# A hybrid S5 / forgetting-attention / mixture-of-experts block: router, sorting step, tail and the down product of the 144-column passes rearranged

## The chip, the cores and the metric

The kernel runs on one core of a Trainium2 chip. The metric is the device time of one execution in microseconds; lower is better. Engines: TensorE (PE, with its weight loads PEld), VectorE (DVE), ScalarE (ACT), GpSimd (POOL) and SyncE (SP), which issues most of the DMAs.

## The reference

For 1024 tokens of width 1024, all in float32:

```python
x = x + concat(rmsnorm(attn), rmsnorm(ssm)) @ w_out          # attention heads and state-space heads
h = rmsnorm(x, norm_ffn_g)
logits = h @ w_router + b_router                             # 32 experts
top_val, top_idx = lax.top_k(logits, 4);  gates = softmax(top_val)
y[e] = (clamped_swiglu(h_rows_of_e @ w_gu[e] + b_gu[e])) @ w_dn[e] + b_dn[e]
x = x + sum over the 4 chosen experts of gate * y
x = x + sigmoid(rmsnorm(x, norm_ple_g) @ w_ple_gate) * (p @ w_ple_proj)
out = rmsnorm(x, norm_final_g)
```

The 4096 (token, expert) rows are grouped by expert; each expert has weights of 8 MB (gate and up) and 4 MB (down).

## The kernel before

The work is written out by hand, engine by engine: each engine has one program, and semaphores (`wait_ge`, `then_inc`) order them. `link` on VectorE and GpSimd makes the next instruction wait for the one before. The stages touched here are these.

**Output projection and router (433 to 570 us).** Eight row tiles `t` of 128 tokens. On TensorE `attn_part` (L1766) and `ssm_part` (L1771) make two 512-column products per half tile, in two PSUM banks; `resid` on VectorE (L1279, L1280) scales each by its row's reciprocal norm and adds it to `x1`, both after `wo_mm`, which the second product signals. `norm_rows` and ScalarE's `ffn_norm` (L806) form the RMS norm and `hn` (L1289). SP stores each `hn` tile to the DRAM table `normalised_rows` (L397) and, for tiles 0 to 5, reads it back in quarters `hq` (L403), from which VectorE's `router_turn` makes the transposed tile `h2T`. Tiles 6 and 7 are transposed on TensorE (`turn_rows`, L1785) and copied by ScalarE (`router_in`, L813). `route` (L1795) multiplies `h2T` as 128-column weights with 128 moving columns of the router weights, placed so that the last 32 are the logits. `logits` (L1293 to L1306) adds the bias, takes the top values and indices and builds the one-hot tiles `oh` and `sel`.

**Sorting step (570 to 616 us).** VectorE counts the rows of each expert (L1343 ff.) and chooses for each a pass width from `WIDTHS = (96, 112, 120, 128, 144, 192, 224, 256)`; `first_ready` gives the first expert to SP, which then loads four of its gate/up chunks (L408). VectorE goes on to each row's place (L1378 to L1391) and makes one-hot tables `ohr`, `ohc` in four quarters (L1395, L1396). ScalarE scales them by token numbers (`tokens_in`, L855) between its other copies (`gates_in` L834, `gates_turned` L841, `bias_out` L847), and TensorE sums them (L1866): the result is the list of row ids. Meanwhile VectorE makes the pass table (L1401 to L1421), which SP copies to `passrow` (L418) for every engine's loop bounds. `rowid` and `rowq` (L1425 to L1427) turn the ids into gather indices; GpSimd gathers the first rows in four indirect DMAs (`gather`, L607); the wait on `rows0_ld` then releases the other gate/up chunks on SP (L437 ff.) and the first turn `xT` on VectorE (L1450). The slot numbers for the final gather (L1432 to L1438) are made ahead of that turn.

**Expert passes (616 to 2103 us).** One loop per width. The passes of 96 (`narrow_pass`) use the tokens as 32-column weights (L1958, L1985), four strips at a time. All others (`expert_pass`) use gate/up weights as the stationary operand and `xT` as the moving one (L1894, or L1897 in 64-column halves up to width 128), and then, for the down product, `actT` as the stationary operand and 512 columns of `wd` as the moving one, for each half `c` all eight `f` (L1911), with a second form for tokens past 128 (L1916, L1924, L1936). There are 6 passes of 96, 8 of 112, 5 of 120, 2 of 128, 7 of 144, 3 of 192 and one each of 224 and 256. VectorE and ScalarE evacuate each `f` (L1497, L1498, L921, L1487, L1490); ScalarE copies the output to `yb` (`y_out`, L876 ff.); GpSimd stores it (`serve_pass`) and gathers rows two passes ahead (`gather_pass`). SP loads each chunk when its predecessor's last reader has signalled `gu_mm` or `dn_mm` (L443 to L450).

**Tail (2103 to 2266 us).** TensorE multiplies the per-layer input (L2023); GpSimd gathers four expert rows per token (L691); VectorE `combine` (L1510) adds them; ScalarE `ple_norm` (L927), TensorE `turn_tail` (L2030), ScalarE `gate_in` (L933), TensorE `gate` (L2039), ScalarE `ple_gate` (sigmoid, L940), VectorE `finish` (L1528, L1529) and `fin_norm` (L944 square, L946 square root) follow, and L1536 makes the output tile. VectorE combines tile `t + 2` ahead of finishing tile `t`.

Of the kernel before, what the change touches and what calls it, by code (L numbers as in the profile page):

```python
# [31 lines left out]
P = 128  # L32
# [13 lines left out]
E = 32  # L46
# [4 lines left out]

GR = 32
# [16 lines left out]
N_SMALL = 1092  # L69
# [36 lines left out]
def build(nc, x_cm, x_tm, pT, small, consts, b_f, d_skipT, b_router, gains, w_in, w_glu, w_out,  # L106
          w_router, w_router_q, w_gu, w_dn, b_exp, b_gu, b_dn, w_ple_gate, w_ple_proj, out, hs, ys, cum):
    with ExitStack() as ctx:
# [166 lines left out]
        slf = at("slf", [P, 32], F32, o); o += 128  # L275
        csel = at("csel", [P, 9, 32], F32, R_V + 32768)
        before = at("before", [1, 32], F32, R_V + 33920)
        assert o <= R_S
# [8 lines left out]
        wd = at("wd", [P, 2, FT, 512], F32, R_H + 65536)  # L287
# [16 lines left out]
        gdT = at("gdT", [P, 2, P], F32, R_S + 32768)  # L304
# [14 lines left out]
        sqj = at("sqj", [P, D], F32, o); o += 4096  # L319
        assert o <= R_C  # L320
# [20 lines left out]
        def _(sp):  # L341
# [89 lines left out]
            def dn_chunk(e, j):  # L431

                sp.dma_start(wd[:, j // 2, 4 * (j % 2):4 * (j % 2) + 4], w_dn[bass.ds(e, 1), j].rearrange("o p f m -> (o p) f m")
                             ).then_inc(S(f"dn_ld{j}"), 16)
# [22 lines left out]
            for t in range(8):  # L457
                sp.wait_ge(S("o_ready"), t + 1)
                sp.dma_start(out[:, t, :], ot[:, t % 2, :]).then_inc(S(f"o_st{t % 2}"), 16)
            sp.wait_ge(S("o_st0"), 64)  # L460
            sp.wait_ge(S("o_st1"), 64)
# [3 lines left out]
        def _(pool):  # L465
# [149 lines left out]

            pool.wait_ge(S("hs_st"), 16 * 8)
            pool.wait_ge(S("first_ready"), 1)
# [3 lines left out]

            pool.wait_ge(S("rowid_ready"), 2)
            gather(0, rowq)
# [26 lines left out]
            def serve_pass(b, narrow):  # L650
# [12 lines left out]
                if narrow:  # L663
                    for j in range(4):
                        pool.dma_start(ys[bass.ds(r0, WIDTHS[0]), 256 * j:256 * j + 256].rearrange("(r t) c -> t r c", t=GR),
                                       yb[GR * j:GR * j + GR, 0, 0:256 * NGR].rearrange("t (r c) -> t r c", c=256)).then_inc(S("y_st"), 16)
                else:
# [12 lines left out]
            with pool.Fori(ends0, npass) as b:  # L680
# [6 lines left out]
            for t in range(8):  # L687
                if t >= 2:
                    pool.wait_ge(S("yg_used"), t - 1)
# [7 lines left out]
        def _(act):  # L697
# [104 lines left out]
            a.activation(rss[:, :], rss[:, :], ACT.Sqrt).then_inc(S("sd2_ready"), 1)  # L802
# [7 lines left out]
            def router_in(t):  # L810
                act.wait_ge(S("ht_mm"), t - 5)
                act.wait_ge(S("ht_evac"), t)
                a.activation(h2T[:, t % 2, :, :].rearrange("p k j -> p (k j)"), ps[:, 4:6, :].rearrange("p b n -> p (b n)"),  # L813
                             ACT.Copy).then_inc(S("ht_evac"), 1)

            for t in range(8):
                ffn_norm(t)
                if t >= 6:
                    router_in(t)
# [7 lines left out]
            act.wait_ge(S("hs_st"), 16 * 8)  # L827
# [42 lines left out]
            def y_out(b, w):  # L870
# [3 lines left out]
                for c in range(2):  # L874
                    act.wait_ge(S("dn_mm"), b * 4 + (2 * c + 2 if rest % P == 0 else 4))
# [41 lines left out]
            for c, w in list(enumerate(WIDTHS))[1:]:  # L917
                with act.Fori(ends[c - 1], ends[c]) as b:
# [3 lines left out]
                    y_out(b, w)  # L922
# [19 lines left out]
            def fin_norm(t):  # L942
                act.wait_ge(S("x3_half"), 2 * t + 2)
                a.activation(sqj[:, :], x1[:, t, :], ACT.Square, accum_out=rstd[:, t:t + 1]).then_inc(S("zs_ready"), 1)  # L944
# [22 lines left out]
        def _(dve):  # L967
# [303 lines left out]
            dve.wait_ge(S("sd2_ready"), 1)  # L1271
# [3 lines left out]
            def resid(t, n):  # L1275
                w = 2 * t + n
                dve.wait_ge(S("wo_mm"), w + 1)
# [851 lines left out]
```

## Time and profile before

| | us |
|---|---|
| median of 3 runs | 2288.71 (2288.33 to 2290.12) |
| the profiled execution's own time | 2268.03 |
| its span, first to last instruction | 2266.5 |
| PE / DVE / ACT / POOL busy | 2208.7 / 958.3 / 423.6 / 605.5 |
| mean granted TensorE clock | 0.994 of full speed |

In the rows "A <- B" in a form reads "tile written <- tiles read", for a matmul "result <- moving, stationary". One float32 matmul of the program is two MATMUL instructions in the trace. `[x <- E]` behind a row of the timeline is idle time of the engine before it and what ended it; a row that begins with two numbers gives start and duration in us.

### The profile page before, as it was taken

How to read it: one execution, taken by the hardware profiler on the slowest of the kernel's cores; microseconds unless marked ns; L12 is line 12 of the kernel's file. 1: busy time of each engine (PE TensorE's matmuls, PEld its weight loads, DVE VectorE, ACT ScalarE, POOL GpSimd, SP SyncE). 2: the span in 40 equal slices, each digit the busy share in tenths (PEclk: the TensorE clock that was granted, in tenths of full speed). 3: DMA queues.
4: the chain of work that ended last, by engine and by line, in shares of the span. 5: the costliest groups of instructions: out<-in, count | busy, mean ns of one | idle time of the engine just before them, and what ended most of it. 6: DMA issues, size and time to landing. Idle time of an engine off the chain costs nothing.

```text
span 2266.5 us, 48298 instructions
## 1 busy us (share of the span) xinstructions
PE 2208.7 (97%) x19138; PEld 1532.9 (68%) x19138; DVE 958.3 (42%) x2120; ACT 423.6 (19%) x873; POOL 605.5 (27%) x915
## 2 busy tenths in 40 slices
PE   8999999999699999999999999999999999999998
PEld 5555566545455577878787787888877888777443
DVE  4664477344743343434344343333332222212474
ACT  3110166301311111111111110111111100010344
POOL 0555588100223312121211212222123111111320
PEclk9999999999899999999999999999999999999999
DMA  5100011321499999999999999788877666543540
GB/s 201 43 25 6 25 56 38 163 74 60 156 405 399 399 408 416 368 353 358 348 339 337 343 330 339 261 317 319 309 293 273 256 250 241 223 159 138 200 155 37
DMA packets 103097, 533.67 MB, mean 235 GB/s; under 512 B 22516, under 2 KB 26404, under 8 KB 50924
## 3 DMA queue, kind: packets, MB, share of 16 engines
q1 hardware_dynamic: 76748, 465.57, 54.4%
q0 software_dynamic: 26272, 67.02, 8.5%
q8 instruction: 55, 0.90, 0.2%
q14 instruction: 22, 0.18, 0.0%
HBM read 498.02 MB, written 31.23 MB: 234 GB/s over the span
## 4 chain that ended last, share of the span: by engine, by line
PE 84%; DVE 6%; DMA 5%; ACT 2%; issue 1%; SPq 1%; POOL 0%; DVEq 0%; POOLq 0%; ACTq 0%
PE ps L1894 20%; PE ps L1897 17%; PE ps L1911 16%; PE ps L1661 5%; DMA wg<-in_w_gu 4%; PE ps L1958 3%; PE ps L1650 2%; PE ps L1771 2%; PE ps L1766 2%; PE ps L1936 2%; DVE x L1510 2%; PE ps L1680 1%; PE ps L1714 1%; PE ps L2039 1%; PE ps L1746 1%
## 5 line engine op out<-in xcount | busy, mean ns | idle before, releaser
L1894 PE MATMUL ps<-xT,wg 128*128 128x144 f32 (+3 forms) x3072 | 451.1, 310 | 0.0
L1894 PEld LDWEIGHTS ps<-xT,wg 128*128 128x128 f32 x3072 | 441.6, 190 | 12.9 <-issue 6.3
L1497 DVE TENSOR_SCALAR gb<-ps,bcur 128x256 f32<-128x256 f32 x216 | 104.6, 484 | 780.2 <-PE ps L1894 458.3
L1897 PEld LDWEIGHTS ps<-xT,wg 128*64 128x64 f32 x7680 | 383.3, 137 | 11.0 <-issue 11.0
L1897 PE MATMUL ps<-xT,wg 128*64 128x112 f32 (+2 forms) x7680 | 386.7, 263 | 0.0
L1911 PE MATMUL ps<-wd,actT 128*128 128x512 f32 x864 | 376.9, 594 | 0.0
L1911 PEld LDWEIGHTS ps<-wd,actT 128*128 128x128 f32 x864 | 162.4, 190 | 196.1 <-issue 188.4
L921 ACT ACTIVATE sg<-gb 128x256 f32<-128x256 f32 x216 | 90.0, 417 | 731.5 <-DVE gb L1497 731.5
L607 POOL DMA_INDIRECT xg<-normalised_rows,rowc x184 | 177.9, 967 | 74.1 <-issue 45.7
L1958 PE MATMUL ps<-wg,xT 128*32 128x256 f32 x2304 | 133.7, 384 | 9.6 <-issue 6.9
L638 POOL COPY rowc<-rowq 128x8 uint32 (+1 forms) x34 | 6.3, 186 | 506.1 <-DVE xT L1450 506.1
L656 POOL DMA_DIRECT2D bin__182<-in_b_exp x33 | 18.9, 574 | 424.6 <-issue 298.1
L2039 PE MATMUL ps<-wpg,xnT 128*128 128x512 f32 x256 | 112.9, 595 | 6.1 <-ACT xnT L933 6.1
L1958 PEld LDWEIGHTS ps<-wg,xT 128*32 128x32 f32 x2304 | 73.3, 111 | 59.5 <-issue 15.2
L876 ACT ACTIVATE yb<-ps 128x512 f32<-128x512 f32 x54 | 31.1, 596 | 408.9 <-PE ps L1911 185.8
L1487 DVE TENSOR_TENSOR tb<-gb,sg 128x256 f32<-128x256 f32 x216 | 91.9, 426 | 34.8 <-ACT sg L921 34.8
L1498 DVE TENSOR_SCALAR ub<-ps,bcur 128x256 f32<-128x256 f32 x216 | 102.7, 475 | 0.0
L1490 DVE SCALAR_TENSOR_TENSOR actT<-ub,tb 128x256 f32<-128x256 f32 x216 | 91.7, 425 | 7.4
L2039 PEld LDWEIGHTS ps<-wpg,xnT 128*128 128x128 f32 x256 | 47.5, 190 | 65.9 <-issue 54.5
L1450 DVE STREAM_TRANSPOSE xT<-xg 128x1024 f32<-128x1024 f32 x61 | 72.4, 1221 | 1.6 <-DMA xg<-normalised_rows,rowq 1.6
L1985 PE MATMUL ps<-wd,actT 128*32 128x256 f32 x1152 | 64.6, 380 | 0.0
L670 POOL DMA_DIRECT2D expert_rows<-yb x48 | 34.9, 732 | 102.4 <-ACT yb L888 63.1
(413 smaller groups left out, 2415.6 us busy)
## 6 DMA issues: line engine op xcount, KB each, us to landing
wg<-in_w_gu SPq DMA_DIRECT2D x264, 1024.0 KB, 7.3
wd<-in_w_dn SPq DMA_DIRECT2D x132, 1024.0 KB, 7.8
expert_rows<-yb POOLq DMA_DIRECT2D x48, 256.0 KB, 8.5
expert_rows<-yb POOLq DMA_DIRECT2D x60, 128.0 KB, 4.8
hT<-in_x_cm SPq DMA_DIRECT2D x8, 512.0 KB, 9.5
cumb<-gate_sums SPq DMA_DIRECT2D x4, 1024.0 KB, 4.6
x<-in_x_tm SPq DMA_DIRECT2D x1, 4096.0 KB, 14.1
wout<-in_w_out SPq DMA_DIRECT2D x1, 4096.0 KB, 21.0
```

The lines of the kernel that those rows point to most:

```text
L607: g.indirect_dma_start(xg[:, half, DQ * r:DQ * r + DQ], None, hs[:, :], bass.IndirectOffsetOnAxis(ap=rows[:, r, half:half + 1], axis=0)).t ...
L921: a.activation(sg[:, f % 2, :], gb[:, f % 2, :], ACT.Sigmoid, scale=1.702).then_inc(S("sig_ready"), 1)
L1487: v.tensor_tensor(tb[:, f % 2, :], gb[:, f % 2, :], sg[:, f % 2, :], ALU.mult).then_inc(S("tb_ready"), 1)
L1490: v.scalar_tensor_tensor(actT[:, f, :], ub[:, f % 2, :], -6.0, tb[:, f % 2, :], ALU.max, ALU.mult).then_inc(S("act_ready"), 1)
L1497: v.tensor_scalar(gb[:, f % 2, :], ps[:, f % 2, 0:W], bcur[:, f:f + 1], 7.0, ALU.add, ALU.min).then_inc(S("g_ready"), 1)
L1498: v.tensor_scalar(ub[:, f % 2, :], ps[:, f % 2, W:2 * W], bcur[:, 8 + f:9 + f], 8.0, ALU.add, ALU.min).then_inc(S("gu_evac"), 1)
L1661: ins = m.matmul(ps[:, bank, :], w_[:, k, un[1] * P:un[1] * P + P], hT[:, k, 512 * un[2]:512 * un[2] + 512], start=(k == 0), stop=(k == KT ...
L1894: ins = m.matmul(ps[:, f % 2, g_ * W:g_ * W + w], wg[:, f, k, g_, :], xT[:, k, 0:w], start=(k == 0), stop=(k == KT - 1))
L1897: ins = m.matmul(ps[c:c + 64, f % 2, g_ * W:g_ * W + w], wg[:, f, k, g_, c:c + 64], xT[:, k, 0:w], start=(k == 0), stop=(k == KT - 1))
L1911: ins = m.matmul(ps[:, 2 + c, :], actT[:, f, 0:P], wd[:, c, f, :], start=(f == 0), stop=(f == FT - 1))
L1958: ins = m.matmul(ps[GR * j:GR * j + GR, ut % 2, 0:256], xT[:, k, GR * r:GR * r + GR], wg[:, f0:f0 + 2, k, j // 2, :], start=(k == 0), stop ...
L2039: ins = m.matmul(ps[:, 2 + n, :], xnT[:, t % 2, k, :], wpg[:, k, n * 512:n * 512 + 512], start=(k == 0), stop=(k == KT - 1))
```

## The change

- **Router.** `wa_mm` is new: `resid` adds the first product when it is done and the second after `wo_mm`. `route` uses the router weights as 32-column stationary tiles in four strips and `h2T` as 128 moving columns; VectorE copies the four partial results (`logit_parts`), and TensorE adds them with a folding matrix (`fold_parts`). `logits` runs one tile later in the order. Tiles 6 and 7 are transposed from `x1`, in halves (`turn_block`); the gain is folded into `wr`, and the row's reciprocal norm is applied at the logits. `hn` of tile 7 is made on GpSimd.
- **Sorting step.** The pass table's arithmetic (L1402 to L1414) goes to GpSimd, which signals `tabs_ready`; its scan (L1401) stays on VectorE, ahead of the sort. ScalarE makes both gate tables before the bias copies. The bias rows' residual is multiplied in before the bias (`rows_in`). Waits for all eight `hs_st` become waits for six on VectorE and ScalarE, and tiles in memory move accordingly. The first gather has three groups; a plain DMA stands in for the fourth. The first turn has three groups too, and the slot numbers come after it.
- **Down product.** `wd` is stored `[P, FT, D]`, with columns in the order (o, r, i) of sizes 8, 4, 32, loaded in pairs of `f`. Passes of 144 use `wd` as the stationary operand and the 144 tokens as the moving one; VectorE transposes the result into `yb` instead of ScalarE's copies, and GpSimd stores 160 rows. All other passes read the moving columns through `down_cols`, and take `f` in the outer loop with both halves inside. VectorE's and GpSimd's pass loops are split in three.
- **Tail.** A dummy square root precedes the square of `fin_norm`; the last tile's square, output and store are made in halves; GpSimd waits for `x2_ready` in place of `yg_used`.

```diff
@@ gpsimd
-            def gather(half, rows):
-                for r in range(4):
+            def gather(half, rows, groups=4):
+                for r in range(groups):
...
+            pool.wait_ge(S("x1_ready"), 8)
+            link(g.tensor_tensor(hn[:, 7, :], x1[:, 7, :], gffn[:, :], ALU.mult))
+            pool.wait_ge(S("rt_evac"), 8)
+            g.tensor_scalar(hn[:, 7, :], hn[:, 7, :], rstd[:, 7:8], 1.0, ALU.mult, ALU.mult).then_inc(S("hn_ready"), 1)
+            pool.wait_ge(S("first_ready"), 2)
+            g.tensor_tensor(cbase[:, :, :], cbase[:, :, :], crow[:, :, :], ALU.subtract)
+            g.tensor_scalar(ctot[:, :], iota[:, 0:NW], pidx, 1.0, ALU.is_equal, ALU.mult)
+            g.tensor_scalar(cown[:, :, :], cnum[:, :, :], pidx, 1.0, ALU.is_le, ALU.mult)
+            link(g.tensor_scalar(cin[:, :, :], cend[:, :, :], pidx, 1.0, ALU.is_gt, ALU.mult))
...
+            pool.sem_inc(S("tabs_ready"), 1)
             pool.wait_ge(S("hs_st"), 16 * 8)
...
+            pool.dma_start(xg[96:P, 0, 3 * DQ:3 * DQ + 32], b_router[96:P, :]).then_inc(S("rows0_ld"), 16)
             pool.wait_ge(S("rowid_ready"), 2)
-            gather(0, rowq)
+            gather(0, rowq, NGR)
@@ scalar
+            act.wait_ge(S("ht_mm"), 2)
+            act.wait_ge(S("ht_evac"), 6)
+            a.activation(h2T[:, 0, :, :].rearrange("p k j -> p (k j)"), ps[:, 4:6, :].rearrange("p b n -> p (b n)"), ACT.Copy).then_inc(S("ht_evac"), 1)
+            for h in range(2):
+                act.wait_ge(S("ht_mm"), 3 + h)
+                a.activation(h2T[:, 1, 4 * h:4 * h + 4, :].rearrange("p k j -> p (k j)"), ps[:, 4 + h, :], ACT.Copy).then_inc(S("ht_evac"), 1)
+                act.wait_ge(S("wo_evac"), 15 + h)
+                if h == 0:
+                    a.activation(sqd[:, 0, :], x1[:, 7, 0:512], ACT.Square, accum_out=ssq[:, :]).then_inc(S("row_sq"), 1)
...
+            for part in range(4):
+                gates_in(1, part)
+            gates_turned(1)
+            act.wait_ge(S("hs_st"), 16 * 8)
             bias_out(0)
+            tokens_in(0)
+            tokens_in(1)
             bias_out(1)
-            for q in range(4):
-                tokens_in(q)
-                gates_in(1, q)
-            gates_turned(1)
+            tokens_in(2)
+            tokens_in(3)
             bias_out(2)
...
             def fin_norm(t):
+                a.activation(sdj[:, :], ones[:, 0:1], ACT.Sqrt)
@@ vector
-            for t in range(8):
+            for t in range(7):
                 resid(t, 0)
                 if 1 <= t < 7:
                     router_turn(t - 1)
                 resid(t, 1)
                 norm_rows(t)
                 if t >= 1:
-                    logits(t - 1)
+                    logit_parts(t - 1)
+                if t >= 2:
+                    logits(t - 2)
+            resid(7, 0)
+            logits(5)
+            logit_parts(6)
+            resid(7, 1)
...
+            logits(6)
+            logit_parts(7)
...
+            logits(7)
...
+                if ws:
+                    dve.wait_ge(S("y_free"), b + 1)
+                    dve.wait_ge(S("dn_mm"), b * 4 + 4)
+                    yt = yb[:, :, :].rearrange("p h (c o i) -> p (h c) o i", c=4, i=32)
+                    yp = ps[:, 2:6, :].rearrange("p k (z c i) -> p c (k z) i", z=2, i=32)
+                    v.transpose(yt[:, 0:4], yp[:, 0:4])
+                    v.transpose(yt[:, 4:5], yp[:, 4:5]).then_inc(S("y_evac"), 1)
@@ tensor
                 for k in range(KT):
-                    at_, lo = (96 - 32 * k, 0) if k < 3 else (0, 32 * (k - 3))
-                    ins = m.matmul(ps[:, 6 + t % 2, at_:at_ + P], h2T[:, t % 2, k, :], (wr if t >= 6 else wrq)[:, :, :].rearrange("p k e -> p (k e)")[:, lo:lo + P],
-                                   start=(k == 0), stop=(k == KT - 1), skip_group_check=True)
+                    j = 32 * (k % 4)
+                    ins = m.matmul(ps[j:j + 32, 6 + t % 2, 0:P], (wr if t >= 6 else wrq)[:, k, :], h2T[:, t % 2, k, :],
+                                   start=(k < 4), stop=(k >= 4), skip_group_check=True)
...
             for t in range(1, 7):
                 project(t + 1, 0)
+                if t >= 2:
+                    fold_parts(t - 2)
                 route(t - 1)
-                if t == 6:
-                    turn_rows(6)
-                project(t + 1, 1)
+                if t < 6:
+                    project(t + 1, 1)
+            turn_block(6, 0)
+            turn_block(6, 1)
+            attn_part(7, 1)
+            fold_parts(5)
             route(6)
-            turn_rows(7)
+            ssm_part(7, 1)
+            turn_block(7, 0)
+            fold_parts(6)
+            turn_block(7, 1)
             route(7)
+            fold_parts(7)
...
+            def down_cols(f, quarter, n):
+                return wd[:, f, :].rearrange("p (o r i) -> p r o i", r=4, i=32)[:, quarter:quarter + n]
...
+                if w == WIDTHS[C_WS]:
+                    for f in range(FT):
+                        if f % 2 == 0:
+                            pe.wait_ge(S(f"dn_ld{f // 2}"), b * 16 + 16)
+                        pe.wait_ge(S("act_ready"), b * FT + f + 1)
+                        for o_ in range(8):
+                            ins = m.matmul(ps[:, 2 + o_ // 2, W * (o_ % 2):W * (o_ % 2) + w], wd[:, f, P * o_:P * o_ + P],
+                                           actT[:, f, 0:w], start=(f == 0 and o_ % 2 == 0), stop=(f == FT - 1), skip_group_check=True)
+                        if f % 2:
+                            ins.then_inc(S("dn_mm"), 1)
+                    return
```

## Rows read from the trace of the kernel before

**Rows 1.** The page, part 1: busy us, share of the span, instructions.

```profile
PE 2208.7 (97%) x19138; PEld 1532.9 (68%) x19138; DVE 958.3 (42%) x2120; ACT 423.6 (19%) x873; POOL 605.5 (27%) x915
```

**Rows 2.** The chain that ended last, in order of time, expert passes: start, us, what.

```profile
643.94 19.29 DMA wg<-in_w_gu
...
1466.59 31.56 PE ps L1894 x256
1498.15 13.73 PE ps L1911 x32
1511.88 3.58 PE ps L1936 x64
```

**Rows 3.** Stretches: length, busy PE, PEld, DVE, ACT, POOL, PEclk, DMA share, GB/s.

```profile
576.00:580.00 4.00, 3.41 (x16) 2.29 (x16) 3.76 (x16) 0.45 (x2) 0.00 (x0) 0.50 0.01 4
628.00:640.00 12.00, 11.86 (x206) 6.64 (x202) 6.50 (x18) 2.08 (x6) 0.00 (x0) 1.00 1.01 421
```

**Rows 4.** The same chain, from the last projection to the first turn.

```profile
558.82 0.76 DVE x L1279
...
564.72 1.03 ACT h2T L813
...
565.80 3.62 PE ps L1795 x16
...
569.52 0.20 DVE lg L1293
...
596.91 0.43 DVE cbase L1402
...
601.35 0.43 DVE tabf L1415
...
603.25 0.19 DVE rowid L1425
...
613.52 1.26 DVE xT L1450
```

**Rows 5.** The same chain: groups of TensorE instructions of three forms.

```profile
139.23 3.55 PE ps L1655 x32
...
549.25 1.78 PE ps L1795 x16
...
635.35 3.59 PE ps L1958 x64
```

**Rows 6.** Groups by line and shape, VectorE and GpSimd: busy us, mean ns, idle before.

```profile
L1088 DVE TENSOR_TENSOR t<-pv_r,par 128x512 f32<-128x512 f32 x4 | 7.1, 1774 | 0.1
...
L1103 DVE TENSOR_TENSOR v_r<-t,t 128x512 f32<-128x512 f32 x4 | 2.8, 692 | 0.1
...
L594 POOL TENSOR_SCALAR sc<-sc,rden 128x256 f32<-128x256 f32 x8 | 3.7, 478 | 0.7 <-DVE rden L1198 0.7
...
L529 POOL TENSOR_TENSOR phi_i<-p,p 128x256 f32<-128x256 f32 x4 | 2.9, 724 | 0.3
```

**Rows 7.** Timeline of the sorting step: last scaling, last gather of the first four.

```profile
597.31 1.24 ACT L855 ACTIVATE ohc<-ohc,cst 128x456 f32<-128x456 f32 x2
...
610.36 0.95 POOL L607 DMA_INDIRECT xg<-normalised_rows,rowq  x1 [0.30 <-issue]
```

**Rows 8.** Timeline and chain of the last pass's output and of the tail.

```profile
2103.25 0.60 ACT L876 ACTIVATE yb<-ps 128x512 f32<-128x512 f32 x1 [12.65 <-PE ps L1916]
...
2212.71 7.13 PE L2039 MATMUL ps<-wpg,xnT 128*128 128x512 f32 x16 [0.87 <-ACT xnT L933]
...
2228.45 7.13 PE L2039 MATMUL ps<-wpg,xnT 128*128 128x512 f32 x16 [0.86 <-ACT xnT L933]
...
2230.37 1.06 ACT L944 ACTIVATE sqj<-x 128x1024 f32<-128x1024 f32 x1 [1.48 <-DVE x L1529]
...
2231.54 1.28 ACT L946 ACT_TABLE_LOAD   x1
...
2236.46 20.62 PE ps L2039 x48
```

More of the change, by code:

```diff
@@ L50 @@
 WIDTHS = (96, 112, 120, 128, 144, 192, 224, 256)
+C_WS = WIDTHS.index(144)
 GR = 32
@@ L68 @@
 O_GATT = 1088
-N_SMALL = 1092
+O_GFFN = 1092
+N_SMALL = 1100
 O_ID, O_TRI, O_IOTA, O_PIDX, O_TID, O_QD, O_MA = 0, 128, 256, 384, 385, 393, 394
@@ L679, in _ @@
                 serve_pass(b, True)
-            with pool.Fori(ends0, npass) as b:
+            ends_ws = [pool.value_load(passrow[0:1, 4 * c + 3:4 * c + 4], min_val=c + 1, max_val=MAXPASS) for c in (C_WS - 1, C_WS)]
+            with pool.Fori(ends0, ends_ws[0]) as b:
+                serve_pass(b, False)
+            with pool.Fori(ends_ws[0], ends_ws[1]) as b:
+                serve_pass(b, False, True)
+            with pool.Fori(ends_ws[1], npass) as b:
                 serve_pass(b, False)
@@ L1319, in router_turn @@
                 turn_32(v, h2T[:, t % 2, :, :], hq[:, t % 2, :]).then_inc(S("ht_evac"), 1)
-            for t in range(8):
+            link(v.tensor_reduce(fold[:, 0, :], ident.rearrange("p (j e) -> p e j", j=4), AX_X, ALU.add))
+            link(v.tensor_copy(fold[:, 1:3, :], fold[:, 0:1, :].to_broadcast([P, 2, 32])))
+            link(v.tensor_tensor(wr[:, :, :], wr[:, :, :], par[:, O_GFFN:O_GFFN + KT].unsqueeze(2).to_broadcast([P, KT, 32]), ALU.mult))
+            for t in range(7):
                 resid(t, 0)
@@ L1331, in _ @@
             link(v.memset(crow[:, :, 32:33], 0.0))
-            logits(7)
             dve.wait_ge(S("ge_ready"), 1)
@@ L1373, in _ @@
             link(v.tensor_reduce(R(4), cbase[:, :, 0:32].rearrange("p c e -> p e c"), AX_X, ALU.add))
+            v.tensor_tensor_scan(fl(cbase), one, fl(crow), 0.0, ALU.mult, ALU.add).then_inc(S("first_ready"), 1)
             sw = RW.unsqueeze(1).to_broadcast([P, 8, 32])
@@ L1478, in _, with wide_pass @@
                 turn_in(0).then_inc(S("xt_evac"), 1)
-            with dve.Fori(ends0, npass) as b:
+            ends_ws = [dve.value_load(passrow[0:1, 4 * c + 3:4 * c + 4], min_val=c + 1, max_val=MAXPASS) for c in (C_WS - 1, C_WS)]
+            def wide_pass(b, ws):
                 dve.wait_ge(S("be_ld"), b * 16 + 16)
@@ L1837, in gates_turn, with rows_in @@
                 ins.then_inc(S("cnt_mm"), 1)
+            def rows_in(r):
+                for j in range(4):
+                    m.matmul(ps[:, 2 + j, :], ident, x1[:, 4 * (r // 2) + j, 512 * (r % 2):512 * (r % 2) + 512], start=True, stop=False,
+                             skip_group_check=True)
             def bias(r, banks, alone):
@@ L1845, in bias @@
                     ins = m.matmul(ps[:, banks[j], :], gdT[32 * j:32 * j + 32, i, :], bdn[32 * j:32 * j + 32, 512 * n:512 * n + 512],
-                                   start=True, stop=alone, skip_group_check=True)
+                                   start=alone, stop=True, skip_group_check=True)
+                    if not alone:
+                        ins.then_inc(S("wo_mm"), 1)
                 if alone:
                     ins.then_inc(S("wo_mm"), 1)
-                else:
-                    for j in range(4):
-                        m.matmul(ps[:, banks[j], :], ident, x1[:, 4 * i + j, 512 * n:512 * n + 512], start=False, stop=True,
-                                 skip_group_check=True).then_inc(S("wo_mm"), 1)
+            rows_in(0)
             gates_turn(0)
-            pe.wait_ge(S("ht_evac"), 9)
+            pe.wait_ge(S("ht_evac"), 10)
             pe.wait_ge(S("out_ld"), 112)
             bias(0, (2, 3, 4, 5), False)
+            gates_turn(1)
             pe.wait_ge(S("wo_evac"), 20)
+            rows_in(1)
             bias(1, (2, 3, 4, 5), False)
```

236 lines of the change are left out of this document (137 added, 99 removed).

## Prediction

> **What bounds the kernel now.** I read the page first, then the chain of waits in order of time, then the stretches, and last the groups by shape. TensorE is busy for 97% of the span [rows 1], so the reader should ask in each stage whether it is TensorE that ends it. Three stages matter here. From the last projection to the first expert pass the chain runs almost wholly through VectorE [rows 4]: time saved on that chain counts. In the six narrow passes that follow, TensorE waits some 19 us in every pass for gate/up weights [rows 2], while the DMA engines are full (share 1.01) [rows 3]. So the narrow passes end at a fixed distance from the moment at which the weight loads resume, and those resume when the first gathered rows land (the wait on rows0_ld in the SP queue, just ahead of the turn at 613.52) [rows 4]. From 823 us to the last pass TensorE is back to back: the only gain there is less TensorE time. In the tail TensorE idles 0.86 us once per tile, waiting for ScalarE [rows 8].
>
> All sums are against the profiled execution, 2268.03 us (span 2266.5 and 1.5 around it). The median of the runs is 2288.71, 20.7 above it; I find nothing in the rows that says where that lies, and carry the difference over unchanged.
>
> **A. Router on TensorE, until the last projection ends.** One router product took 1.78 us [rows 5]. The new form has 16 instructions on 32 columns, four strips side by side. Bounds: the four-at-once row with 512 columns took 3.55 us for 32 instructions, so a quarter of the columns and half the count could give 0.45; the other end is no gain, 1.78. The nearest row is the narrow pass, 3.59/64 = 56 ns an instruction [rows 5], the lowest that any row shows: 0.9, and I add 0.1 for the change of shape: 1.0. The fold is one matmul of 96 columns: 0.2. Ahead of the last projection's end stand now seven routes and six folds, 8.2, in place of six routes, 10.7: **-2.5** (from -6 to +3). The halved residual adds let VectorE start before the second product; TensorE does not wait there, so they are worth 0.8 once, counted in B. The fold's preparation on VectorE, three small operations ahead of the first add, is hidden: TensorE needs the first bank back only after two more products.
>
> **B. From the last projection (558.82) to the last logits (569.52), 10.7 us [rows 4].** Before: two residual adds 1.5, square and normalisation 3.2, turn 1.1, copy 1.0, route at half clock 3.6. Now the tile is turned unnormalised in halves. After the projection: one add 0.8, turn 0.5, ScalarE's copy of the second half, delayed by its first copy and square to 2.6; route 1.0; copy, fold and latency 0.5; then VectorE's mean, square root on ScalarE, reciprocal 0.7: 4.8. **-5.9** (-4 if the route stays at half clock, -7 if everything meets).
>
> **C. GpSimd's two operations for row tile 7.** The second (1.1 us, one input) starts when the last index is found and meets VectorE's two-input compare: **+0.7** (0 to 1.1). The first meets logits(6), which has that slack. The store of tile 7 and, behind it on SP's queue, the bias loads come some 3 us later than they would; TensorE needs them 3 us after that.
>
> **D. The pass table on GpSimd.** It takes L1402 to L1414, 596.91 to 601.35, off VectorE: 4.4 us [rows 4]. On GpSimd it starts near 581, while VectorE sorts. A GpSimd product or sum of 256 takes 0.72, a one-input operation 0.48 [rows 6]; nine of the first, three of the second and small ones make 8 us, ready near 592, before the sort ends: no wait at tabs_ready. But the rows show a price. A VectorE product of 512 took 1774 ns in the stretch where GpSimd multiplies, against 692 for the same shape alone [rows 6]: each lost about 0.85 to a GpSimd operation of its own size. The Trainium skill (SBUF — State Buffer, Who interferes with whom) says that a VectorE instruction with two SBUF inputs and a GpSimd one that reads SBUF exclude each other for a whole instruction; by that rule, the trace agrees. It speaks against this part. Halved for 256 columns, and with some three of the twelve falling on VectorE's reductions and casts, nine meetings at 0.4 give 3.5 us (0 to 5.4). Then the last one-hot quarter is ready at 596.2 + 0.3 (memsets moved behind the last logits) + 0.6 (scan moved forward) + 3.5 = 600.7. ScalarE now has a bias copy of 2.5 us between the second and third quarter, then 2.5 us for two scalings (1.24 each) [rows 7], and TensorE its last quarter, 1.8: row ids at 604.5 in place of 603.25 [rows 4]: **+1.3**. Without the contention it is 601.3, -1.9; if TensorE's last quarter also runs at half clock, as TensorE did at 576 to 580 [rows 3], it is +3.
>
> **E. First gather.** One of four indirect gathers goes, each 0.95 with 0.30 between [rows 7]: **-1.25**. The added DMA is issued before the wait for row ids, and lands first. The slot arithmetic, moved behind the first turn, takes 4.3 us of VectorE; TensorE fills two banks, 2 x 3.59 at the least [rows 5], before it needs the first one back, so it is covered; uncovered it would cost up to 4.3.
>
> The loads resume 2.5 + 5.9 - 0.7 - 1.3 + 1.25 = **7.7 us earlier** (3 to 13).
>
> **F. Down product in the passes of 144.** Before: 13.73 + 3.58 = 17.31 [rows 2]. Now 64 matmuls with 128x128 weights and 144 moving columns, the very shape of the gate product, which takes 31.56 for 128: 15.78. -1.53 in seven passes: **-10.7**. The evacuation moves to VectorE, two transposes of 1.25 and 0.4 us behind a wait for the down product. Queued behind it are the next pass's first evacuations, which TensorE feeds 3.9 us later: hidden. In the other passes the down product keeps its counts, with the same columns read in runs of 32: 0 (rival 3).
>
> **G. Last pass.** The output copies of the first half no longer overlap: four of 0.60 after the last matmul in place of two [rows 8]: **+1.2**, on the way to both the projection matmuls and the final gathers.
>
> **H. Tail.** A dummy square root draws the table load (1.28) ahead of the square, into ScalarE's idle 1.48 [rows 8]. The ScalarE/VectorE loop falls from 15.74 (2212.71 to 2228.45) to 14.5. TensorE needs 16 x 2 x 0.43 + 0.87 = 14.6 and becomes the bound: -1.13 in five tiles, **-5.6** (-3 to -5.7). Behind it, 20.62 of TensorE stays. At the end the load goes too, but the half squares queue behind it, and the last output goes out in halves: **-1.0** (0 to -2).
>
> Sum: -7.7 - 10.7 + 1.2 - 5.6 - 1.0 = **-23.8**: 2244.2 profiled, 2264.9 as a median; I say 2265.
>
> **Rivals.**
> 1. The engines do not block each other on these small operations, and the strips run near their column time: D gives -1.9 and C 0, A -6, so 3.9 + 3.5 more: 2257. For it: the blocked rows have 512 columns, none of 256 does. Against: the size of the loss follows the operation's length. Chance 0.17.
> 2. The earlier start is lost: half clock in the one-hot products, the contention in full, and routes no faster (A +3, D +3): the start moves by 0.5 only, 2272. The same number results if the narrow passes do not pass the shift on. For it: half clock stands in [rows 3] at just this place. Chance 0.15.
> 3. **Slower than before.** The moving rows of the down weights are no longer contiguous: runs of 32 values (128 bytes) with gaps of 384. No row shows a moving operand of this kind; the nearest, in the narrow pass, has two runs of 128 and pays nothing [rows 5]. Outside the passes of 144 there are 672 instructions of 512 columns at 429 ns and, for the remainders of the last passes, some 70 such lengths more: about 740. The gain of 23.8 is gone at 32 ns each, 7.5% of their time. At 15% it is 47 us: 2312. Chance 0.05. The Trainium skill (SBUF — State Buffer, Door 1: The DMA port swizzle) speaks of 16-byte lines as the grain of an access; runs of 128 bytes fill them whole, and no run here shows it.
> 4. The 144 change gives nothing (eight interleaved sums in four banks cost 24 ns a matmul): 2276. Against: the gate product of that shape. Chance 0.06.
>
> **How the numbers follow.** Forecast 0.57; its own range, from the bounds above, is 2259 to 2272. To hold 8 in 10 the range takes in most of rivals 1 and 2 and reaches to 4: 2255 to 2277. A change of 0.2% (4.6 us) is about what a measurement can tell. Slower: rival 3 and a little for a stall I do not see, 0.05; within 0.2%: partial forms of 3 and 4, 0.03; faster 0.92.
>
> **What would show it.** A: route groups of 1.0 us. B: last logits 4.8 after the last projection. D: the sort's two-input operations at 0.8 in place of 0.43 while GpSimd works, table ready before the sort ends. E: first turn 7.7 earlier, at 605.9. F: passes of 144 at 47.3 in place of 48.87. H: tail period 14.6, no idle before TensorE. Wrong would be: 512-column down matmuls above 429 ns, a wait of VectorE at tabs_ready, narrow passes longer than 34.2.

## The result, and the profile after

| | before | after | ratio, 95% interval |
|---|---|---|---|
| first set of runs, median us | 2289.41 (4 runs) | 2265.53 (4 runs) | 0.9893 (0.9878 to 0.9909) |
| second set (e5), median us | 2268.43 (7 runs) | 2241.82 (4 runs) | 0.9880 (0.9864 to 0.9897) |
| profiled execution shown first | 2268.03 | 2265.32 | |
| profiled again (e1, e5): span | 2265.8 | 2240.0 | |

The change takes 24 to 27 us off. But the two profiles that came first differ by 2.7 us only. The profile of before lies 21 us below the runs of its set; the one of after agrees with its own. Read naively, that pair says that the change did nothing. So the first thing to find was where 21 us sit that one profile has and the other lacks.

The page of the first profile after, part 1, beside [rows 1]:

```profile
PE 2201.0 (97%) x19378; PEld 1592.8 (70%) x19378; DVE 972.0 (43%) x2134; ACT 406.0 (18%) x844; POOL 620.0 (27%) x932
```

Its waits of TensorE (line, waited for, us in total, times, longest) in three stretches: 645 to 827, 1180 to 1420 and 1470 to 1800 us.

```profile
PE ps L2111 <- issue: 3.9, 6, 0.8
...
PE ps L2020 <- issue: 0.6, 1, 0.6
...
PE ps L2017 <- issue: 6.0, 13, 1.1
```

And its timeline around the end of one pass of 144 columns (start, us, engine, line, what, idle before):

```profile
1469.87 0.28 PE L2017 MATMUL ps<-xT,wg 128*128 128x144 f32 x1
1470.60 0.19 PEld L2017 LDWEIGHTS ps<-xT,wg 128*128 128x128 f32 x1 [0.78 <-issue]
1470.61 0.38 PE L2017 MATMUL ps<-xT,wg 128*128 128x144 f32 x1 [0.46 <-issue]
1471.33 2.84 PE L2017 MATMUL ps<-xT,wg 128*128 128x144 f32 x21 [0.34 <-issue]
1471.59 1.25 DVE L1584 STREAM_TRANSPOSE yb<-ps 128x1024 f32<-128x1024 f32 x1 [13.12 <-remote]
```

"issue" means that TensorE waits for nothing that a semaphore shows. Behind every pass of 144 it stands still at one or two places among its next instructions, here 0.46 and 0.34 us; a pass takes 48.47 us, 1.4 more than its two products. In every narrow pass there are such gaps inside the third strip of `rows_out`, and these passes take 36.1 us. The new down product itself has nearly the forecast length, 15.68 us. If the gaps belonged to the changed code, F would be worth 7 x 0.4 = 2.8 us (48.47 against 48.87) and not 10.7. The experiments begin there.

### The profile page after: what moved, and what is told of

It is laid out like the page before. It is cut to its first block, busy times and chain, and to the rows that moved or that the text cites. A ratio compares the mean times of both kernels' runs of the same rounds, so it can differ in the third digit from the quotient of the medians.

```text
span 2263.7 us, 48831 instructions
## 1 busy us (share of the span) xinstructions
PE 2201.0 (97%) x19378; PEld 1592.8 (70%) x19378; DVE 972.0 (43%) x2134; ACT 406.0 (18%) x844; POOL 620.0 (27%) x932
## 4 chain that ended last, share of the span: by engine, by line
PE 91%; DVE 3%; issue 2%; ACT 2%; POOL 1%; DMA 1%; POOLq 0%; DVEq 0%; SPq 0%; ACTq 0%
PE ps L2017 20%; PE ps L2020 17%; PE ps L2045 13%; PE ps L2084 6%; PE ps L1758 5%; PE ps L2033 5%; PE ps L2111 3%; PE ps L2163 3%; PE ps L1863 2%; PE ps L1747 2%; PE ps L1869 2%; PE ps L1709 1%; PE ps L1843 1%; PE ps L1742 1%; PE ps L1777 1%
## 5 line engine op out<-in xcount | busy, mean ns | idle before, releaser
L2045 PE MATMUL ps<-wd,actT 128*128 128x512 f32 x672 | 293.2, 594 | 0.0
L2045 PEld LDWEIGHTS ps<-wd,actT 128*128 128x128 f32 x672 | 126.4, 190 | 153.5 <-issue 152.3
L2084 PEld LDWEIGHTS ps<-wg,xT 128*32 128x32 f32 x2304 | 84.5, 111 | 46.1 <-issue 10.5
L2033 PE MATMUL ps<-actT,wd 128*128 128x144 f32 x896 | 110.9, 286 | 0.0
L2033 PEld LDWEIGHTS ps<-actT,wd 128*128 128x128 f32 x896 | 110.2, 190 | 0.0
L2111 PE MATMUL ps<-wd,actT 128*32 128x256 f32 x1152 | 74.8, 381 | 5.3 <-issue 3.9
L926 ACT ACTIVATE yb<-ps 128x512 f32<-128x512 f32 x40 | 21.8, 595 | 304.1 <-PE ps L2045 208.3
## 6 DMA issues: line engine op xcount, KB each, us to landing
x<-in_x_tm SPq DMA_DIRECT2D x1, 4096.0 KB, 13.8
```

The lines of the kernel that those rows point to most:

```text
L2033: ins = m.matmul(ps[:, 2 + o_ // 2, W * (o_ % 2):W * (o_ % 2) + w], wd[:, f, P * o_:P * o_ + P], actT[:, f, 0:w], start=(f == 0 and o_ % 2 ...
L2045: ins = m.matmul(ps[:, 2 + 2 * h + c, :], actT[:, f, P * h:P * h + P], down_cols(f, 2 * c, 2), start=(f == 0), stop=(f == FT - 1))
L2084: ins = m.matmul(ps[GR * j:GR * j + GR, ut % 2, 0:256], xT[:, k, GR * r:GR * r + GR], wg[:, f0:f0 + 2, k, j // 2, :], start=(k == 0), stop ...
L2111: ins = m.matmul(ps[GR * j:GR * j + GR, 2 + r // 2, 256 * (r % 2):256 * (r % 2) + 256], actT[:, f, GR * r:GR * r + GR], down_cols(f, j, 1) ...
```

## The experiments

### e1: the kernel before, profiled again

No edit.

> The kernel before once more, unchanged, for a second profiled execution. Its first profile took 2268.03 us beside a median of 2288.7, 20.7 us less, and the narrow passes in it take 34.2 us each with TensorE waiting only for weight loads (0.6 us in 5 passes). Theory: an ordinary run pays those 20.7 us somewhere, and a second profile that comes out near 2288 shows the place; I expect the seven narrow passes, 2 to 3 us each (36.1 us per pass, as in the profile after), and the same 31.56 + 17.31 us in the passes of 144. Rival: the profile again takes about 2268 and the difference stays invisible. Timed against itself: ratio 1.000, within 0.15%.

Measured: 2268.24 us, against 2268.0 for the same kernel, ratio 1.0001 (0.9992 to 1.0011). Not 2289: the rival of the expectation came true. In this and all later sets the kernel before takes what its first profile took (2268.0 to 2268.9). The narrow passes are again 34.2 us each, the passes of 144 again 31.56 + 13.73 + 3.58. So the profiles of before go with the later sets, and the first set of runs was taken in other circumstances.

### e2: passes of 144 in the old form

```diff
-                if w == WIDTHS[C_WS]:
+                if False:
...
-                    if c != C_WS:
-                        y_out(b, w)
+                    y_out(b, w)
```

and VectorE's and GpSimd's loops for 144 as for the other widths.

> The changed kernel with the passes of 144 columns back in the old form (activations stationary, down weights moving, evictions on ScalarE, four stores of 256 KB), all else as changed. The profile after shows 15.68 us for the new down product as forecast, but 1.42 us of gaps named issue at the head of each following pass, so that a pass costs 48.47 instead of 48.87 us. Theory, the profile holds: taking the new form away costs 7 x 0.4 = 2.8 us, 2268.3. Rival, the prediction's term holds in ordinary runs: it costs 10.7 us, 2276. Second rival, the down weights' new layout makes the old form slow as moving rows with a stride: over 2280.

Measured: 2254.97 us. Against after in the same circumstances (e5, 2241.82) the old form costs 13.1 us. The numbers expected started from 2265; as differences they are +2.8, +10.7 and over +15. The first rival holds: outside the first set F is worth its full term, and 2.4 us more. The other widths keep 13.93 us for 32 instructions of 512 columns over the rearranged down weights, to the last digit what they were; the layout costs nothing.

### e3: fewer signals, e4: shifted program, e5: after once more

e3 gathers the `dn_mm` increments as follows, and in the passes of 144 puts all four on the last matmul:

```diff
-                        if r == NGR - 1 and f % 2:
+                        if r == NGR - 1 and f == 3:
                             ins.then_inc(S("dn_mm"), 1)
+                    if r == NGR - 1:
+                        ins.then_inc(S("dn_mm"), 3)
```

e4 puts increments at the head of TensorE's program:

```diff
             pe.wait_ge(S("ones_ready"), 1)
+            for _ in range(128):
+                pe.sem_inc(S("passed"), 1)
```

> The changed kernel with the down products' semaphore signals gathered: in the narrow passes one after four features' groups and the other three with the last matmul, as in the kernel before, instead of one after every second; in the passes of 144 all four with the last. The profile after has gaps named issue of about 2.3 us in each narrow pass between the groups of the third strip, where the kernel before had none, and 1.42 us behind each pass of 144. Theory A, the signals make the gaps: both vanish, -7 x 1.9 and -7 x 1.4 us, about 2242. Theory B, the place of the instructions in TensorE's program makes them: gaps stay about as they are, 2265, within 2 us.

> The changed kernel with 128 semaphore increments more (127 instructions of 64 bytes in the compiled program) at the head of TensorE's program, where it waits for its first data; every later instruction lies 8128 bytes further on, and nothing else changes. Theory B, the place of the instructions makes the gaps: they move to other instructions, vanish or grow in the narrow passes and behind the passes of 144, and the time changes by several us either way. Theory A, the signals make them: the same gaps at the same instructions, 2265.5 within 2 us.

> The changed kernel once more, unchanged. In the first set of runs the kernel before took 2268.0 us, as in its first profile, not 2289. Theory C: the gaps named issue in the first profile after (1.9 us in each narrow pass, 1.42 us behind each pass of 144) belong to the circumstances of those runs, in which the kernel before paid 20.7 us more too, and not to the kernel; here they are gone, narrow passes take 33.5 us where no weight load is waited for, the passes of 144 31.56 + 15.68 = 47.2 us, and the time is 2242 to 2245 (0.9893 x 2268.0 = 2243.7), as e3_fewer_signals. Theory A, the signals make the gaps: they are there again and the time is about 2264, 22 us above e3_fewer_signals.

Measured: e3 2241.83, e4 2252.39, e5 2241.82 us. e3 came out at the very number that theory A had named, and both kinds of gap were gone. Without e5 that would have passed for proof. e5 is the control: the same program as the first profile after takes the same time as e3 and has no gaps either. So neither the signals nor the place of the instructions is enough to make them, and A and B, each taken alone, fall. e4 has no gaps, its narrow and 144 passes are those of e5, and its 10.6 us come from the head, where TensorE's first matmul stands behind the increments. The same row in e4, then in e5 (waits of TensorE, 0 to 40 us):

```profile
PE ps L1711 <- DVE hT L1178: 20.8, 1, 20.8
```

```profile
PE ps L1709 <- DVE hT L1178: 8.7, 1, 8.7
```

The row names `hT`, but VectorE had finished its first part at 8.5 us in both profiles; it is the increments that hold TensorE until 20.8.

Theory C holds: the gaps go with the first set of runs. Whether signals or place have a part in the circumstances of that set was not tried, since e3 and e4 ran outside them. Nor is the first set's chip on record, while the later sets ran on three different ones and agree; so a chip of its own, or anything else that was different then, stays possible. Loads of instructions do not explain the gaps at 1518.7 and 1519.4 us in the first profile: no packet of an instruction queue moves in it between 1471.3 and 1519.8 us. The chain of waits of e5, in order of time, the first two passes of 144 and the one after:

```profile
1408.84 31.36 PE ps L2017 x256
1440.20 15.68 PE ps L2033 x128
1455.88 31.36 PE ps L2017 x256
1487.24 15.68 PE ps L2033 x128
1502.92 31.36 PE ps L2017 x256
```

A pass takes 47.04 us with nothing between, where the first profile had 48.47. Over the seven that is 10.0 us, and the six narrow passes were 13.8 us longer there (609.42 to 827.35, against 610.17 to 814.26): together as good as all of the 23.7 us between 2265.5 and 2241.8. That before lost its 21 us in the same places is a guess: no profile of before was caught in those circumstances.

### e6: reads of the pass ends first

```diff
-            pe.wait_ge(S("wo_evac"), 28)
             pe.wait_ge(S("tab_ld"), 16)
             ends = [pe.value_load(...) for c in range(NW)]
+            pe.wait_ge(S("wo_evac"), 28)
```

> The changed kernel with TensorE's nine reads of the pass table's ends moved ahead of its wait for the last evictions of the bias product (wo_evac 28); that wait comes after them. In the profiles the first narrow pass starts 6.24 us after those evictions both before and after, 5.3 us of it named issue, and 6.3 us after the first turn. Theory: the pass starts 4 to 5 us earlier, about 605.5 where the turn is done at about 604.5, but the weight loads are not moved, and the narrow passes end with waits for them, so the time falls by under 1.5 us. Rival, TensorE bounds the narrow passes: -4 to -5 us.

### e7: pass table back on VectorE

The block from `cbase - crow` to `tabs_ready` leaves GpSimd; VectorE gets L1402 to L1414 of the kernel before, behind the one-hots.

> The changed kernel with the pass table's products back on VectorE behind the one-hots, in the form of the kernel before; all else as changed. Prediction's term: GpSimd's products beside VectorE stretch its operations of 0.85 us and under and cost 1.8 (measured in the profile after) to 3.5 us (forecast) on the way to the row ids, so row ids come 1.8 to 3.5 us earlier; the table comes after them, some 5 us later than now, and is needed by the value reads of GpSimd's gather and SyncE only at the first turn. Theory: -1.5 to -3 us in all. Rival, the later table holds up TensorE's reads of the ends and the loads of the first passes: +2 to +5 us. Second rival: 0, as the gather is not what the first pass waits for.

### e8: up weights requested early

```diff
-            for f in range(4):
+            for f in range(FT):
                 gu_chunk(e0, f)
             sp.wait_ge(S("tab_ready"), 1)
...
             sp.wait_ge(S("rows0_ld"), 64)
-            for f in range(4, FT):
-                gu_chunk(e0, f)
```

> The changed kernel with the first expert's chunks 4 to 7 of the up weights (4 MB) requested directly behind chunks 0 to 3, ahead of the pass table, instead of behind the first gather; they land at about 595, where the queues are idle from 584 to 604. The narrow passes' loads then run some 10 us ahead. Theory, the weight loads set the end of the narrow passes: TensorE no longer waits for a load in passes 5 and 6 (0.7 us each) and the time falls by 1 to 2 us. Rival: the loads delay the table and the first gather by a few us, +2 to +5.

Measured: e6 2241.06, e7 2240.12, e8 2240.73 us; against e5 -0.8, -1.7 and -1.1. The runs of one kernel in this set spread over 0.6 to 2.1 us, so that e6's -0.8 is hardly clear of noise by itself; the traces carry the reading. The start of the narrow passes in the timelines of e5, e6, e7 and e8:

```profile
596.01 0.28 DVE L1497 COPY rowid<-ps 128x114 f32<-128x114 f32 x1 [2.15 <-PE ps L1985]
603.99 0.98 DVE L1515 STREAM_TRANSPOSE xT<-xg 128x768 f32<-128x768 f32 x1 [3.43 <-DMA xg<-normalised_rows,rowq]
604.13 2.09 SPq L416 DMA_DIRECT2D wg<-in_w_gu  x4
610.17 2.36 PE L2084 MATMUL ps<-wg,xT 128*32 128x256 f32 x20 [8.17 <-issue]
```

```profile
604.11 2.08 SPq L416 DMA_DIRECT2D wg<-in_w_gu  x4
605.40 6.90 PE L2084 MATMUL ps<-wg,xT 128*32 128x256 f32 x124 [3.36 <-DVE xT L1515]
```

```profile
593.87 0.27 DVE L1493 COPY rowid<-ps 128x114 f32<-128x114 f32 x1
601.96 2.12 SPq L416 DMA_DIRECT2D wg<-in_w_gu  x4
608.16 4.07 PE L2080 MATMUL ps<-wg,xT 128*32 128x256 f32 x48 [8.30 <-issue]
```

```profile
610.39 1.94 PE L2082 MATMUL ps<-wg,xT 128*32 128x256 f32 x16 [8.30 <-issue]
```

Then the chains where they leave the narrow passes, in e5, e6, e7 and e8:

```profile
771.35 19.64 DMA wg<-in_w_gu
...
814.26 24.68 PE ps L2020 x512
```

```profile
605.68 13.56 DMA wg<-in_w_gu
...
702.62 19.75 DMA wg<-in_w_gu
...
736.98 19.58 DMA wg<-in_w_gu
...
771.17 19.72 DMA wg<-in_w_gu
...
814.17 24.68 PE ps L2020 x512
```

```profile
812.26 24.68 PE ps L2016 x512
```

```profile
813.67 24.68 PE ps L2018 x512
```

In e6 TensorE starts 4.8 us earlier and leaves the narrow passes at the same moment: it now waits for weights in four passes, 5.0 us in all and 3.2 of them in the first, where e5 has one wait of 0.5. The loads resumed at 604.1 in both. In e7 they resume 2.2 us earlier, TensorE starts 2.0 earlier, and the passes end 2.0 earlier; since both moved, e7 does not tell the two bounds apart. In e8 no chain entry is a load any more, and the end is TensorE's: 203.3 us from its start. From the moment the loads resume to the end it is 209.9 us in e1, 210.1 in e5 and e6, 210.3 in e7. That is the prediction's premise, shown from both sides: the loads set the end, and TensorE's own work lies less than 1 us behind.

e7 also prices the contention. VectorE's sort in e5, and the same operations in e7 (timeline, VectorE):

```profile
576.36 1.02 DVE L1470 SCALAR_TENSOR_TENSOR smp<-rt,prf 128x256 f32<-128x256 f32 x1
...
580.30 0.65 DVE L1474 TENSOR_SCALAR psi<-psi 128x32 int32<-128x32 int32 x1
...
581.07 0.62 DVE L1476 CAST pcr<-psi 128x64 f32<-128x64 int32 x1
581.72 1.81 DVE L1480 TENSOR_TENSOR ohr<-pcr,cst 128x1024 f32<-128x1024 f32 x1
```

```profile
575.30 0.42 DVE L1454 SCALAR_TENSOR_TENSOR smp<-rt,prf 128x256 f32<-128x256 f32 x1
...
578.48 0.18 DVE L1458 TENSOR_SCALAR psi<-psi 128x32 int32<-128x32 int32 x1
...
578.78 0.20 DVE L1460 CAST pcr<-psi 128x64 f32<-128x64 int32 x1
579.01 1.22 DVE L1464 TENSOR_TENSOR ohr<-pcr,cst 128x1024 f32<-128x1024 f32 x1
```

Ten operations of the sort are longer in e5, by 4.1 us in sum. The last one-hot is ready at 592.1 in e5 and 587.7 in e7. Of the 4 us only 2.1 reach the row ids, because VectorE now makes the table ahead of copying them. GpSimd lost time as well: its share of the table took 13.3 us in e5 (572.3 to 585.6) where D had 8. It was hidden all the same, since it was ready before the sort ended.

### e9: the three together, e10: product late, e11: no dummy root

e9 has the three edits above. e10 adds:

```diff
             pool.wait_ge(S("x1_ready"), 8)
+            pool.wait_ge(S("rt_evac"), 8)
             link(g.tensor_tensor(hn[:, 7, :], x1[:, 7, :], gffn[:, :], ALU.mult))
-            pool.wait_ge(S("rt_evac"), 8)
```

e11 is after without `a.activation(sdj[:, :], ones[:, 0:1], ACT.Sqrt)`.

> The changed kernel with the edits of e6, e7 and e8 together: reads of the ends ahead of the wait, the pass table back on VectorE, up weights 4 to 7 requested ahead of the table. Alone they gave -0.8, -1.7 and -1.1 us. Theory: each was held back by the other bound (in e6 TensorE started 4.8 us earlier and then waited for loads in three passes, in e8 the loads were ahead and TensorE was the bound from 610.4 us on). Together TensorE starts at about 603.2 and, with no wait for loads, needs the 203.3 us of e8 to the end of the narrow passes: 806.5, 7.8 us earlier than in e5, so 2241.8 - 7.8 = 2234. Rival, the gains only add up: 2238.2. Second rival, loads and the early pass meet and the waits come back: 2240.

> As e9_three_together, but GpSimd's product for row tile 7 (2.36 us) starts only when the last index is found, directly ahead of its scaling, instead of beside VectorE's work on the second last logits, where a conversion took 1.20 in place of 0.17 us. Theory: VectorE gives back 1.0 us there, and loses as much or more behind it, where product and scaling now stand beside compares and products of two inputs on the way to the gates (0.29 to 0.61 us each), so the time against e9 is between 0 and +1.5 us. Rival, a meeting behind the last index costs nothing more: -1.0 us.

> The changed kernel without ScalarE's dummy square root ahead of each tile's last square in the tail; all else as changed (halved last output included). Prediction's term: the table load of 1.28 us falls back onto the way between square and square root, the loop of ScalarE and VectorE takes 15.7 us a tile instead of 14.9, and in five to six tiles that is +4 to +5.6 us, plus up to 1 us at the end: about 2247. Rival, the waits for the gathers or TensorE hide the load: +0 to +1 us.

Measured: e9 2233.77 us, ratio to before 0.9840 (0.9827 to 0.9853), 8 us better than after: more than the 3.6 that the three gave singly, as e6 and e8 had each been stopped by the other bound. TensorE starts at 603.25 and enters the first pass of 112 at:

```profile
806.10 24.68 PE ps L2014 x512
```

e10 2236.02 us, +2.2 against e9, more than the 0 to 1.5 expected. In the two profiles 0.5 of it stands ahead of the edit (last residual add at 555.06 against 554.57), 1.3 between that add and the gates, and the rest behind them, where no experiment looked. The timeline of e10 shows the 1.3, a loss of 2.1 less the 1.0 given back, and small ones:

```profile
560.20 2.34 POOL L626 TENSOR_TENSOR hn<-x,gffn 128x1024 f32<-128x1024 f32 x1 [146.94 <-DVE i L1343]
560.29 2.40 DVE L1348 TENSOR_TENSOR oh<-idxf,cst 128x128 f32<-128x128 f32 x1
```

A VectorE compare of 128 elements, 0.29 us alone, took 2.40, since GpSimd's product had started 0.09 us before. In e5 the victim was a conversion, 1.20 against 0.17 us, while GpSimd's product ran from 555.63 to 557.99:

```profile
556.82 1.20 DVE L1365 CAST idxf<-i 128x4 f32<-128x4 uint32 x1
```

Both victims end within 0.2 us of GpSimd's product: what is lost is the rest of its instruction, however short the victim. The Trainium skill (SBUF — State Buffer, Who interferes with whom) says that VectorE and GpSimd share one pair of ports to SBUF, that whoever issues first has it for the whole instruction, and that the other blocks fully. By that rule, the trace agrees.

e11 2246.64 us, +4.8: the dummy root is worth most of the tail's term. Without it a table load stands again behind the square, as in [rows 8], and the loop of ScalarE and VectorE takes 15.8 us a tile; in e5 it is 14.9 (gates at 2158.79 and 2188.59, two tiles):

```profile
2158.79 7.13 PE ps L2163 x16
...
2188.59 7.13 PE ps L2163 x16
```

### e12: before, a third time

> The kernel before a third time, for a profile, in case this run falls into the circumstances of the very first set (before 2289, after 2265.5). Theory C: if it comes out near 2289, its narrow passes show gaps named issue as the first profile after did, some 2 us each, and further ones in the passes of 144; if it comes out near 2268 it repeats e1 (narrow passes 34.2 us, passes of 144 48.9 us) and the question stays open.

Measured: 2269.18 us against 2268.43, ratio 1.0002 (0.9991 to 1.0013). The circumstances of the first set did not return, and what they were stays open.

## Why the prediction was right, step by step

Total: -23.8 forecast; -23.9 and -26.6 measured in the two sets. The agreement to 0.1 us in the first set is luck: where the steps can be measured they come to -25.8, and their misses, up to 1.9 us, partly cancel. The two spans of e1 and e5 can be taken apart. e1's marks are 433.50 (first projection), 612.94 (loads resume), 822.86 (narrow passes end), 1417.44 and 1759.32 (passes of 144) and 2102.7 (last expert matmul); e5's are 433.80, 604.13, 814.26, 1408.84, 1738.12 and 2081.35.

| step | forecast us | measured us |
|---|---|---|
| upstream, not of the change | 0 | +0.3 |
| A router until the last projection | -2.5 | -4.2 |
| B to the last logits | -5.9 | -5.3 |
| C to the gates | +0.7 | +0.7 |
| D to the row ids | +1.3 | +1.8 |
| E row ids to the loads | -1.25 | -2.1 |
| loads resume, narrow passes end | -7.7 | -8.8, -8.6 |
| F passes of 144 | -10.7 | -12.6 |
| other passes | 0 | -0.2 |
| G and H together | -5.4 | -4.5 |

**The premise of the narrow passes** was right, but I misread the row under it. I wrote that TensorE waits some 19 us in every pass for weights. 19 us is the length of the load that the chain runs through; TensorE computes for nearly all of it. Its own waits there, in the kernel before (us in total, times, longest):

```profile
PE ps L1958 <- DMA wg<-in_w_gu: 2.6, 5, 0.6
```

So the loads set the end by a margin of 2.6 us, not of 19 a pass. The earlier end was passed on because TensorE's start moved too, from 616.20 to 610.17, and its way from there took 204.1 us instead of 207.1. Had only the loads been moved, the gain would have stopped at TensorE's bound, as in e8. The reserve was small, and I did not know it.

**A** was undersized. I took the 56 ns of the narrow passes as the pace of a strip instruction and added 0.1 us; a route took 0.57 us in e5, 36 ns an instruction. With half the moving columns the strips do not keep the old pace. Part of it comes back behind the route, where the next projection takes 3.63 us instead of 3.44. The chain of e5 in one tile, where [rows 5] had 1.78:

```profile
486.21 0.20 PE ps L1899 x2
486.40 0.57 PE ps L1892 x16
486.98 3.63 PE ps L1863 x8
```

**B** is short by the sentence in C that "the first meets logits(6), which has that slack". It had none: the conversion it blocked for 1.03 us stands ahead of `logit_parts(7)` on VectorE's queue, and the last fold waited for that copy, not for the route. Of the 5.3 us some 3.0 are the last route itself. Before, it took 3.62 us at a granted clock of 0.54 (565.8 to 569.4), for the most part the lower of its two levels, 1.2 GHz, after TensorE had been idle for 3.0 us ahead of its turn and 1.1 ahead of the route; in e5 it takes 0.64 at 1.00, the upper level, 2.4 GHz, with 0.3 and 0.7 us of idle time ahead. **C** and **D** hold in the main: 3.5 us forecast for the meetings of D, 4.1 measured. But the sum was not sound in itself. The two rows named for the price differ by 1.08 us (1774 and 692 ns) and not by 0.85, which would have made nine meetings cost 4.9. And the meetings were wrong in kind. I counted two-input operations; shifts and conversions with one input were held up as well (0.65 against 0.18, 0.62 against 0.20), the reduction over `ohp` not (1.22 in both), and some two-input ones not either (L1466 0.43 in e5).

**E** got 0.85 us that no term had. In e1 the second gather took 1.80 us beside two fills of VectorE, the others 0.95 to 1.07; in the new order it takes 0.97. The timeline of e1:

```profile
606.36 0.91 DVE L1431 MEMSET yb<- 128x1024 f32 x1 [0.35 <-DVE xg L1430]
606.59 1.80 POOL L607 DMA_INDIRECT xg<-normalised_rows,rowq  x1 [0.30 <-issue]
607.18 0.36 DVE L1432 TENSOR_TENSOR cmask<-cmask,cbase 128x256 f32<-128x256 f32 x1
```

The same fill stands beside the second gather of e5 in the same way, and there the gather takes 0.97:

```profile
599.64 0.91 DVE L1503 MEMSET yb<- 128x1024 f32 x1 [0.35 <-DVE xg L1502]
599.88 0.97 POOL L617 DMA_INDIRECT xg<-normalised_rows,rowq  x1 [0.30 <-issue]
```

So the fill alone does not hold it. What is left is the slot arithmetic behind the fill, which the change moved away; that is argued, as no run moves it by itself.

**F** is the new shape at the old shape's pace, 15.68 us, plus a bonus: behind the old form's tiles of 16 stationary columns the next up product took 31.56 us, behind the new form 31.36. The eviction is hidden as said. **G and H** miss by 0.9. G holds: from the last expert matmul to the first gate product it is 31.0 us in e1 and 31.9 in e5. H is short: the tile loop stays at 14.9 us and not TensorE's 14.6; in four tiles TensorE still waits for ScalarE's copy, 2.4 us in all. Table loads for root and sigmoid still alternate in every tile, and in e5's chain several of them stand; that they are what is missing is argued.

Rival 1 was right in part about the strips (-6 where A had -2.5; -4.2 came, about midway) and wrong about the blocking. Rival 2 falls with the marks of e1 and e5: the loads resume 8.8 us earlier and the passes end 8.6 earlier. Rival 3 falls with 13.93 us for 32 instructions in both kernels. Rival 4 looked true in the first profile after and falls with e2 and e5. That profile also showed one of the prediction's signs of being wrong, narrow passes longer than 34.2 us; in e5 they take 33.5. One premise passed by luck: I carried 20.7 us over unchanged without knowing where it lay. It came out so because both kernels pay about the same in the first set, 21 and 24 us. With a profile and runs from different circumstances, only differences within one set mean anything.

## What to carry to other kernels

Where loads set the end of a stage and compute lies just behind, moving either alone gives almost nothing; price them together (0.8, 1.7 and 1.1 us singly, 8.0 together). In the two meetings of e5 and e10 with GpSimd's product of 2.4 us, a short VectorE operation lost the rest of that product (1.0 and 2.1 us), not a share of its own length: keep long GpSimd operations away from chains of short ones on VectorE. A load on the chain is not a wait of the engine: read the engine's own waits beside it. And no edit explains a difference until the unchanged kernel has been run beside it.

## What was not expected of the hardware

- Gaps of TensorE named issue, of 0.3 to 1.1 us at fixed places of a loop, in one set of runs and in none of the later profiles of the same or nearly the same program; 24 us of 2265. The same program has them once and once not; the cause is open.
- A strip instruction with 128 moving columns has a pace of 36 ns, with 256 columns 56 ns (four strips at once).
- A moving operand in runs of 32 values costs nothing against contiguous ones (13.93 us for 32 in both).
- 128 semaphore increments in a row held TensorE's first matmul until 20.8 us. Their condition was met at 1.3 us, which leaves up to 0.15 us each, an estimate; 8.7 us of it were hidden behind the wait for the first data, and 10.6 were paid.
- TensorE's reads of the pass ends took some 5 us of issue time ahead of the first narrow pass; moved ahead of a wait (e6), they let it start 4.8 us earlier.
